# Two transformer blocks in fp32 on one core: the part ahead of the experts staged anew

## The reference: what is computed

```python
def first_block(x, c, ctx, c_ctx, w_mod, ...):
    sh1, sc1, gt1, sh2, sc2, gt2 = split(silu(c) @ w_mod + b_mod, 6)       # w_mod is 1024 x 6144
    csh1, csc1, ... = split(silu(c_ctx) @ w_mod + b_mod, 6)                # of these only csh1, csc1 are used
    hx = rms_norm(x, norm1_g) * (1 + sc1) + sh1                            # 256 tokens
    hc = rms_norm(ctx, norm1_g) * (1 + csc1) + csh1                        # 256 context tokens
    q, gb, gc, u = columns of hx @ w_in;  k, v = columns of [hc; hx] @ w_in
    q, k = rms_norm per head of 64, then axial rope on the part from x
    a  = softmax(q k^T / 8) v                                              # 8 heads, 2 kv heads, 512 keys
    cv = gb * conv3(gc * u)
    x  = x + gt1 * (concat(head_rms(a), head_rms(cv)) @ w_out)
    h  = rms_norm(x, norm2_g) * (1 + sc2) + sh2
    x  = x + gt2 * hier_moe(h)           # router: one of 4 groups, 2 of its 8 experts; 32 experts of 1024x768x1024
    return rms_norm(x, final_g)
# second_block: c @ w_ada, a SwiGLU feed-forward (2816), projections, latent and chunk attention, w_out, feed-forward
```

## Time and profile before the change

| | us |
|---|---|
| median of 3 runs | 1654.09 (1653.45 to 1655.84) |
| the profiled execution | 1657.84 |
| its span, first to last instruction | 1656.1 |
| TensorE busy in the span | 1534.6 (93%) |
| VectorE busy | 565.9 (34%) |
| ScalarE busy | 330.4 (20%) |
| mean DMA rate | 290 GB/s |

### The profile page before, as it was taken

The page is one execution under the profiler, slowest core; times in us unless marked ns, Lnnn a source line. Parts: engine busy times, 40 slices in busy tenths (PEclk is TensorE's granted clock), DMA queues, the critical chain, the costliest instruction groups (busy, mean ns, idle before and its releaser), DMA issues.

```text
span 1656.1 us, 22332 instructions
## 1 busy us (share of the span) xinstructions
PE 1534.6 (93%) x9534; PEld 1079.2 (65%) x9534; DVE 565.9 (34%) x982; ACT 330.4 (20%) x530; POOL 23.0 (1%) x31
## 2 busy tenths in 40 slices
PE   6997689999999999999999789999789999899996
PEld 4784475444444444444444479999677767799996
DVE  4747632111111110111111175555435263355553
ACT  2202221111111111111111132222200041244441
POOL 0002000000000000000000000000100000000000
PEclk9897888999999999999999999999989999999997
DMA  9870457999999999999999968777386500345440
GB/s 371 342 256 1 174 240 311 428 432 434 433 432 433 431 433 428 432 432 433 433 433 432 376 233 291 261 271 261 104 336 231 201 1 25 129 153 203 173 157 25
DMA packets 124504, 480.32 MB, mean 290 GB/s; under 512 B 6316, under 2 KB 53673, under 8 KB 108081
## 3 DMA queue, kind: packets, MB, share of 16 engines
q1 hardware_dynamic: 120896, 476.99, 71.8%
q10 hardware_dynamic: 3121, 1.18, 0.3%
q0 software_dynamic: 448, 1.59, 0.3%
HBM read 478.68 MB, written 1.06 MB: 290 GB/s over the span
## 4 chain that ended last, share of the span: by engine, by line
PE 71%; DMA 20%; DVE 5%; ACT 2%; ACTq 1%; issue 1%; SPq 0%; DVEq 0%
DMA arena<-in_w_up_dram 18%; PE psum L870 16%; PE psum L1196 16%; PE psum L1123 13%; PE psum L1217 8%; PE psum L1142 5%; PE psum L1107 2%; PE psum L1089 2%; PE psum L886 1%; DMA arena<-in_w_in_dram 1%; PE psum L969 1%; PE psum L1010 1%; PE psum L1021 1%; PE psum L895 1%; PE psum L904 1%
## 5 line engine op out<-in xcount | busy, mean ns | idle before, releaser
L1123 PE MATMUL psum<-arena,squares 128*64 128x384 f32 x2048 | 337.9, 487 | 19.4 <-DMA arena<-in_w_up_dram 14.6
L1123 PEld LDWEIGHTS psum<-arena,squares 128*64 128x64 f32 x2048 | 145.9, 137 | 213.5 <-issue 181.5
L1720 DVE TENSOR_TENSOR mixT<-mixT,psum 128x384 f32<-128x384 f32 x32 | 26.4, 827 | 489.2 <-PE psum L1123 489.2
L870 PE MATMUL psum<-hT,arena 128*128 128x256 f32 (+1 forms) x784 | 174.5, 385 | 11.8 <-DMA arena<-in_w_in_dram 10.3
L870 PEld LDWEIGHTS psum<-hT,arena 128*128 128x128 f32 (+1 forms) x784 | 150.3, 193 | 34.2 <-DMA arena<-in_w_in_dram 10.7
L1142 PE MATMUL psum<-arena,small 128*64 128x512 f32 x768 | 171.9, 597 | 0.0
L1142 PEld LDWEIGHTS psum<-arena,small 128*64 128x64 f32 x768 | 52.4, 137 | 95.9 <-issue 94.0
L1196 PE MATMUL psum<-ff_x_hi,ff_w_hi 128*128 128x256 f32 x704 | 106.4, 293 | 8.8 <-ACT ff_x_hi L678 8.8
L1765 DVE TENSOR_TENSOR ff_w_lo<-arena,ff_w_hi 128x2048 fp32r<-128x2048 f32 x44 | 100.8, 2291 | 16.8 <-ACT ff_w_hi L770 15.3
L1196 PEld LDWEIGHTS psum<-ff_x_hi,ff_w_hi 128*128 128x128 f32 x704 | 93.7, 192 | 12.5 <-issue 9.5
L1382 DVE SCALAR_TENSOR_TENSOR mod_acc<-arena,cond,mod_acc 128x512 f32<-128x512 f32 x133 | 100.0, 752 | 4.7
(11 more groups left out here) (265 smaller groups left out, 1404.2 us busy)
## 6 DMA issues: line engine op xcount, KB each, us to landing
arena<-in_w_gate_dram SPq DMA_DIRECT2D x32, 3072.0 KB, 31.6
arena<-in_w_up_dram SPq DMA_DIRECT2D x32, 3072.0 KB, 33.9
arena<-in_w_down_dram SPq DMA_DIRECT2D x32, 3072.0 KB, 31.6
arena<-in_ffn_w_in_dram SPq DMA_DIRECT2D x44, 1024.0 KB, 7.1
arena<-in_w_ada_dram SPq DMA_DIRECT2D x18, 2048.0 KB, 11.7
arena<-in_w_mod_dram SPq DMA_DIRECT2D x12, 2048.0 KB, 16.2
arena<-in_w_in_dram SPq DMA_DIRECT2D x11, 2048.0 KB, 13.8
arena<-in_ffn_w_out_dram SPq DMA_DIRECT2D x22, 1024.0 KB, 4.8
```

The lines of the kernel that those rows point to most:

```text
L870: last = pe.matmul(dst, lhsT=lhs[i], rhs=rhs[i], start=(i == 0), stop=(i == n - 1))
L1123: last = pe.matmul(b[64 * half:64 * half + 64, 0:HALF_E], lhsT=xeT[:, k, u * SLOTS:(u + 1) * SLOTS], rhs=w[:, k, half * HALF_E:(half + 1) ...
L1720: nc.vector.tensor_tensor(hidden.rearrange("q (c p) -> q p c", c=3), gate_act.rearrange("q (p c) -> q p c", c=3), bank[5][:, 0:HALF_E].rea ...
```

## The change

- **Row norms.** ScalarE squares the token rows as they arrive, with `accum_out`, giving one sum per token (`token_sums`, 128x4). Root and reciprocal are of 128x4; TensorE spreads them to all partitions (`spread_x`, `spread_ctx`: 2 matmuls each). `sum_x` and `sum_ctx` go.
- **Modulation.** `w_mod` arrives in pieces of 256 rows by 2048 columns. `piece` adds up 8 matmuls per piece in one bank; after four pieces one copy and one turn (`turn_pieces`, 4 matmuls) give 16 columns. The eight late pieces are read one per attention step; the last copy and turn come behind attention. All five VectorE items, their `col_job`s and the three row jobs go.
- **Load order.** All of `w_in` is loaded before the late pieces; then `w_out0`, gate 0 and up 0 of the experts, `w_out1`, up 1 and down 1 (once `mg_ready` is full), down 0, gate 1.
- **Order on TensorE.** `z_gb`, `qk_sum`, `z_gc`, `qk_rot`, `z_u`, attention. VectorE takes the jobs in the same order.
- **Head norms.** `head_sums` gives one column per head and token block in a 128x32 tile; root and reciprocal are of 128x32, and 32 matmuls spread them into banks 4 to 7.
- **Router.** The token rows are copied by ScalarE from banks 4 to 7; `bias_turn` moves to the start, and VectorE's position angles now stand ahead of the first modulation columns.
- **Middle.** `w2_lat` is the first entry and goes to slot 4, `ada14` to slot 5; both no longer wait for `ffn1_sum_done`, only for the last `ada` item. Slots 0 to 3 wait for it one by one.

```diff
-PRE = ([(f"mod{i}", f"modrow{i}") for i in range(4)]
-       + [("w_kv", "z_v"), ("gt1a", 0), ("w_q", "z_q1"), ("gt1b", 1), ("w_gb", "z_gb1"), ("sh2a", 2), ("w_gc", "z_gc1"),
-          ("sh2b", 3), ("w_u", "z_u1"), ("sc2a", 4), ("sc2b", "row_sc2b"), ("gt2a", "row_gt2a"), ("gt2b", "row_gt2b"), ("w_out0", "merge1"),
-          ("w_out1", "merge3")])
+PRE = ([(f"mod{i}", i + 1) for i in range(N_MOD_PIECES)]
+       + [("w_kv", "z_v"), ("w_q", "z_q1"), ("w_gb", "z_gb1"), ("w_gc", "z_gc1"), ("w_u", "z_u1")]
+       + [(f"late{i}", N_MOD_PIECES + i + 1) for i in range(7)] + [("w_out0", "merge1"), ("late7", N_MOD_PIECES + 8), ("w_out1", "merge3")])
...
+            if part == "mid":
+                s = (at + 4) % RING if at < 13 else (2, 3, 5, 4)[at - 13]
...
-            for s in range(3):
+            for s in range(2):
                 wait_item_read(sp, readers[s])
             load_gate(0, 0)
+            wait_item_read(sp, readers[2])
             load_up(0, 0)
-            for s in range(3, RING):
-                wait_item_read(sp, readers[s])
-            readers.clear()
-            load_down(0, 0)
+            load_w_out("w_out1", "merge3")
             sp.wait_ge(sem("mg_ready"), KD)
-            load_gate(1, 1)
             load_up(1, 1)
             load_down(1, 1)
+            for s in (3, 4):
+                wait_item_read(sp, readers[s])
+            load_down(0, 0)
+            wait_item_read(sp, readers[5])
+            load_gate(1, 1)
...
-                sp.wait_ge(sem(f"{key}_sum_done"), 1)
                 readers.clear()
+                for s in range(4):
+                    readers[s] = f"{key}_sum_done"
...
+            def piece(name, b, condition, first, last):
+
+                ring_arrived("pre", name)
+                i = int(name[-1]) % 4
+                w = ring(PLACE[("pre", name)][0]).rearrange("p (k n) -> p k n", k=2)
+                for k in range(2):
+                    for m in range(4):
+                        done = pe.matmul(b[32 * m:32 * m + 32, :], lhsT=condition[:, 2 * i + k, :], rhs=w[:, k, 512 * m:512 * m + 512],
+                                         start=first and k == 0, stop=last and k == 1, skip_group_check=True)
+                done.then_inc(sem("pieces_read"), 1)
...
+            for i in range(2):
+                piece(f"mod{i}", bank[4], cond, i == 0, False)
+            pe.wait_ge(sem("token_rstd_ready"), 1)
+            for at, what in ((0, "x"), (2, "ctx")):
+                b = open_job(f"spread_{what}")
...
+            for i in range(2, 4):
+                piece(f"mod{i}", bank[4], cond, False, i == 3)
+            turn_pieces("mod_turn", 1)
...
+                    if i == 0:
+                        pe.wait_ge(sem("job_emptied"), done_jobs[0])
+                    if key == "at1" and i < n:
+                        piece(f"late{i}", bank[1], cond_late[:, :, 1 - i // 4:33 - i // 4], i == 0, i == n - 1)
+                    if key == "at1" and i == n + 2:
+                        head_sums((4, 5, 6, 7, 0, 1), 1)
...
-            pe.wait_ge(sem("mg_squares"), 1)
-            for i in range(4):
-                b = open_job(f"head_sum{i}")
-                close_job(pe.matmul(b[:, :], lhsT=K("heads64"), rhs=squares[:, 2 * i:2 * i + 2, :], start=True, stop=True))
-            row_job("pre", "row_gt2b", "gt2b", cond)
-            turn_row_job("col_gt2b", 0, "row_gt2b")
+            head_sums((2,), 2)
+            head_sums((3,), 3).then_inc(sem("mg_sums"), 1)
+            turn_pieces("late_turn", 2)
+            pe.wait_ge(sem("mg_rstd"), 1)
+            for c in range(KD):
+                for tb in range(2):
+                    for h in range(2):
+                        at = 16 * tb + 2 * c + h
+                        last = pe.matmul(mg_spread(c)[64 * h:64 * h + 64, tb * P:(tb + 1) * P],
+                                         lhsT=head_rstd[:, 1, at:at + 1].broadcast_to((P, 64)), rhs=ident, start=True, stop=True,
+                                         skip_group_check=True)
```

## The result

| us | before | after |
|---|---|---|
| median (lowest to highest, 4 runs each) | 1653.77 (1651.40 to 1655.84) | 1640.42 (1639.34 to 1641.19) |
| the profiled execution | 1657.84 | 1641.19 |
| its span | 1656.1 | 1639.4 |

The ratio is 0.992, 95% interval 0.9904 to 0.9937. The change makes the kernel 13.4 us faster. The forecast was 44.9 us, a time of 1609.2 and a range of 1600 to 1626: far too large a gain. The medians of before and after differ by 13.4, the two profiled executions by 16.7; what follows adds up the second. Each profile is of one execution; where that matters, it is said.

What follows compares the result with a forecast made beforehand. DMA bytes bound the expert loop; ahead of it TensorE and engines waiting in a row set the pace, plus one middle gap. Savings of 38.2 before expert 0 and 6.7 in the middle gave 44.9: 1609.2 us, range 1600 to 1626.

Steps and rivals of the forecast that it cites:

- Step 1: Start up to z_k: z_k at 38.5 us instead of 39.6, 1.1 saved (-1.0 to +2.1).
- two things that could end last: Start: by the weights' last piece z_k comes at 37.9 us, by VectorE's position angles at 38.9.
- a little faster: Start: if the pieces' longer rows move a little faster, z_k comes at the lower bound, 37.5 us.
- Rival F: Whole kernel: some wait keeps the old order, so a third of the gain, 1640 us; chance 0.03.
- Step 2: z_k to attention, 104.3 us before: projection work of 76.1 stays, waits and low clock go; 28.2 saved (25 to 29).
- Step 3: Attention to first merge, 52.3 us before: longer steps with pieces, shorter head-norm tail; 2.4 saved (-6 to +5).
- Rival A: Low clock stays in projections (3 to 5 us), merges (2.5) and z_lat (2); time 1618; chance 0.18.
- Steps 4, 5 and 6: Merges at full clock, 2.5 us saved; router's shorter VectorE chain, 4.0; middle with earlier w2_lat and z_lat, 6.7.
- The loop is moved, not changed: Expert loop: weights are all in by 201 us, so it starts 38.2 earlier with its length unchanged.
- The stretch behind the loop: Last gate load to the first feed-forward's last sum: forecast change 0.

Runs made afterwards that it cites:

- r1: The changed kernel with the six small loads (router, bias rows) issued by GpSimd instead of ScalarE; 1629.4 us, ratio 0.9846.
- r7: The changed kernel with three edits together: small loads on GpSimd's queue, VectorE's angles behind the first norm's scaling, head sums 128 columns wide; 1625.7 us, ratio 0.9832.
- r9: r7 plus 128 bytes of padding ahead of the big weight buffer; 1617.0 us, ratio 0.978.
- r11: The changed kernel with only the four relative-bias loads issued from GpSimd's queue instead of ScalarE's; 1629.2 us.
- r13: The changed kernel with only the router's two loads issued from GpSimd's queue, the relative-bias loads staying on ScalarE; 1627.6 us (2 runs).
- r3: The changed kernel with VectorE's position angles put back behind the first norm's scaling; 1638.7 us, ratio 0.9907.
- r5: The kernel before with only the change's edit of the middle (load order, slots and waits); 1646.5 us, ratio 0.9974.
- r4: The changed kernel with the head sums' 16 matmuls made 128 columns wide instead of 2; 1637.3 us, ratio 0.9904.
- r10: r9 plus TensorE multiplying zeros in three idle stretches between expert loop and first feed-forward block; 1611.6 us, ratio 0.9749.

## Why the prediction was wrong, step by step

**Step 1 failed, and it is half of the miss.** It weighed two things that could end last, weights and VectorE's angles, and left out ScalarE: the wait for its issues was put at nothing, although rows 4 show one relative-bias issue of 5.48 us among others of 0.7. The runs showed 11.35 us of waiting for ScalarE and `z_k` at 53.43 instead of 38.5. The pieces' longer rows were in the sum only as "a little faster". The bytes came 1.2 to 2.5 late: in r1, r7, r9, r11 and r13 the last piece starts at 33.4 to 34.7 (forecast 32.2), and `z_k` at 39.7 to 42.2 (38.5, upper bound 40.6). The late end of that range has the low clock in it, which the step left out too: the last piece takes 3.64 in r11 and 1.93 in r9. The second thing, the angles, was named rightly, and cost 4.4 (r3) once ScalarE had made everything late. Rival F, some wait keeps the old order, gave 1640 with a chance of 0.03. It has the time but not the mechanism: the order is new, and a new wait is in front of it.

**Step 2 held in what it built, not in what it saved.** The new stretch takes 76.3 for 76.1: the norm chain hides behind `z_gc`, the rotations cover the bank. But the 28.2 saved count the low clock of `z_q` as something that the change takes away, and r5 has that stretch without it: against its profile 24.7 are saved. The -28.0 in the table agrees so well because it is read from the same profile as the forecast. The sum then took off this profile's 3.75 over the median as if the changed kernel's profile would lie as far above its own; it lies 0.8 above. So the time missed by 31.2 (1640.4 against 1609.2) and not by 28.2.

**Step 3** was right in what it called its least-known term: steps of 4.96 for 5.05, pieces of 1.92, no drain from one tiling mode more. It failed in the tail, 11.5 for 7.8 from the last values on; the steps ahead came out 0.8 late. Spreading at full clock is 3.71 (r4) for 4.3; the head sums, costed at 0.24 each at full clock, let the clock fall. Rival A had the right kind of cost, and put it in the projections and the merges instead.

**Steps 4, 5 and 6 held:** 2.4, 3.7 and about 7 for 2.5, 4.0 and 6.7; the last is 6.7 in r5 by itself.

**"The loop is moved, not changed" failed by 4.3 us,** by something that is in no stage: 1392 bytes of new small tensors move the buffer off a multiple of 256.

**The stretch behind the loop** was held to be the same; it isn't by 4.3 us, of which it stays open whether the change has any part. Rival A had the low clock "stay with" the start, merges and `z_lat` only.

With the causes taken out (r9), the profiled execution's span is 1613.1, where the forecast had 1612.9 less the 1.7 around it: 1611.2. That is partly luck: it is the fastest execution of r9 beside a slow one of the kernel before. By the medians r9 gains 36.4 (1653.5 to 1617.0), not 44.9.

## What to carry to other kernels

Before rows of a load are made longer, look at what other engines issue at the same time: two DMA queues take turns packet by packet, so small packets left at 52 a microsecond beside 8 KB ones and at 183 beside 2 KB ones, and the engine that issued them did nothing else until the last was issued. Issued by GpSimd, which had nothing to do then, they held nobody up (r1). Here ScalarE's operations stand behind its DMA issues in program order, so a sum over a start has a term for each engine that issues. Small tensors in front of a large load buffer were not free: 128 bytes off a multiple of 256 cost 4.3 us of the loop. Sums of two columns looked cheaper than sums of 128 and weren't, since the work behind them ran at the low clock. And before a stretch's length is taken from one profile, look at a second execution: a forecast that counts its low clock as saved counts chance.

## What the runs showed of the hardware

- Packets of two queues alternate one for one (914 and 914, 262 and 262 from 15 to 20 us), at 2 KB and at 8 KB alike. Both queues together moved 387 GB/s with the 2 KB rows and 405 with the 8 KB rows.
- An issue of 128 packets takes 0.5 us (r13); with the router's 2048 packets ahead on the same engine, one of four takes 5.5 us beside 2 KB rows and 16.3 beside 8 KB ones.
- The same loads run at 432 GB/s (300 to 800 us) into a buffer at a multiple of 256 bytes, and at 429 when it starts 128 bytes off: 606.4 to 606.6 us for the loop in five profiles, 610.2 to 611.1 in ten.
- TensorE, busy without a gap, fell to 1.2 GHz behind 24 instructions of two columns each; with 128 columns it did not (r4, r7, r9, r10).
- The same code, with the same waits, ran at either clock from one execution to the next: `z_q` 16.64 us in the profile before and 14.03 in r5.
